# Turning q, k and y1 by 32x32 blocks on VectorE and by way of DRAM, in place of TensorE's transposes

## The reference

```python
def pool_layer(x, norm_g, w_in, w_pool, pool_scale, w_out):
    h = rms_norm(x, norm_g)
    u, z = jnp.split(h @ w_in, 2, axis=-1)
    y = pool_mixer(u, w_pool, pool_scale) * jax.nn.silu(z)
    return x + y @ w_out

def moba_layer(x, norm_g, w_in, q_norm, k_norm, w_out):
    h = rms_norm(x, norm_g)
    q, k, v, z = jnp.split(h @ w_in, 4, axis=-1)
    q = rope(rms_norm(heads(q), q_norm))
    k = rope(rms_norm(heads(k), k_norm))
    v = heads(v)
    o = moba_attention(q, k, v).transpose(0, 2, 1, 3).reshape(B, S, D_INNER)
    return x + (o * jax.nn.silu(z)) @ w_out
```

## Time and profile before

| | us |
|---|---|
| median of 3 runs | 430.5 (430.43 to 430.61) |
| the profiled execution | 432.63 |
| its span | 430.8 |
| TensorE (PE) busy | 423.2 |
| VectorE (DVE) busy | 285.3 |
| ScalarE (ACT) busy | 230.6 |
| GpSimd (POOL) busy | 128.4 |

### The profile page before, as it was taken

How to read it: one execution, slowest core, us unless ns; L and a number is a source line. 1 busy time by engine, 2 the same in 40 slices (tenths; PEclk the granted TensorE clock), 3 DMA queues, 4 the chain that set the end, 5 groups by cost and what they waited for, 6 DMA issues and landing times.

```text
span 430.8 us, 5669 instructions
## 1 busy us (share of the span) xinstructions
PE 423.2 (98%) x2214; PEld 363.1 (84%) x2214; DVE 285.3 (66%) x354; ACT 230.6 (54%) x406; POOL 128.4 (30%) x97
## 2 busy tenths in 40 slices
PE   6999999999999999999999999999999999999997
PEld 6989898988888888888878888888888888888885
DVE  1979987779875545356664798447983579836532
ACT  3935553535354443478448765577654786546310
POOL 0157000000000000079904595055940559300000
PEclk9999999999999999999999999999999999999999
DMA  8986869464555747436933567336672355731002
GB/s 271 384 282 214 272 207 342 160 210 142 195 196 153 227 129 218 124 92 208 300 111 99 173 183 236 93 98 194 192 213 86 98 196 195 241 108 43 2 0 97
DMA packets 38026, 75.25 MB, mean 175 GB/s; under 512 B 1648, under 2 KB 1776, under 8 KB 38000
## 3 DMA queue, kind: packets, MB, share of 16 engines
q1 hardware_dynamic: 37280, 73.83, 53.0%
q10 hardware_dynamic: 720, 1.07, 0.7%
HBM read 73.84 MB, written 1.05 MB: 174 GB/s over the span
## 4 chain that ended last, share of the span: by engine, by line
PE 89%; POOL 7%; DMA 2%; ACT 1%; DVE 0%; issue 0%; ACTq 0%
PE acc L579 23%; PE acc L581 23%; PE acc L580 23%; PE aux L634 3%; POOL wide L326 3%; PE acc L602 3%; PE acc L624 3%; PE acc L621 3%; PE acc L623 3%; PE aux L718 2%; DMA wide<-in_xT_dram 2%; POOL k_s L319 1%; PE aux L725 1%; PE aux L737 1%; PE aux L736 1%; PE aux L735 1%
## 5 line engine op out<-in xcount | busy, mean ns | idle before, releaser
L816 DVE TENSOR_TENSOR w_lo<-raw,w_hi 128x2048 fp32r<-128x2048 f32 x65 | 160.2, 2470 | 55.9 <-ACT w_hi L349 55.8
L349 ACT ACTIVATE w_hi<-raw 128x2048 fp32r<-128x2048 f32 x64 | 122.1, 1917 | 40.4 <-PE acc L581 27.6
L579 PE MATMUL acc<-w_hi,hT_hi 128*128 128x512 f32 x320 | 127.7, 399 | 0.0
L581 PE MATMUL acc<-w_hi,hT_lo 128*128 128x512 f32 x320 | 125.0, 391 | 0.0
L580 PE MATMUL acc<-w_lo,hT_hi 128*128 128x512 f32 x320 | 124.8, 390 | 0.0
L581 PEld LDWEIGHTS acc<-w_hi,hT_lo 128*128 128x128 f32 x320 | 60.1, 188 | 12.9
L580 PEld LDWEIGHTS acc<-w_lo,hT_hi 128*128 128x128 f32 x320 | 60.3, 188 | 11.6
L579 PEld LDWEIGHTS acc<-w_hi,hT_hi 128*128 128x128 f32 x320 | 60.2, 188 | 11.5
L579 PE MATMUL acc<-w_hi,aT_hi 128*128 128x512 f32 x160 | 63.7, 398 | 0.0
L581 PE MATMUL acc<-w_hi,aT_lo 128*128 128x512 f32 x160 | 62.5, 391 | 0.0
L580 PE MATMUL acc<-w_lo,aT_hi 128*128 128x512 f32 x160 | 62.4, 390 | 0.0
(11 more groups left out here) (125 smaller groups left out, 568.4 us busy)
## 6 DMA issues: line engine op xcount, KB each, us to landing
raw<-in_w_in_dram SPq DMA_DIRECT2D x46, 1024.0 KB, 5.4
raw<-in_w_out_dram SPq DMA_DIRECT2D x16, 1024.0 KB, 5.0
raw<-in_w_pool_dram SPq DMA_DIRECT2D x4, 1024.0 KB, 5.5
raw<-in_w_in_dram SPq DMA_DIRECT2D x8, 256.0 KB, 8.0
wide<-in_xT_dram ACTq DMA_DIRECT2D x4, 256.0 KB, 7.6
xs<-in_x_dram SPq DMA_DIRECT2D x1, 1024.0 KB, 8.5
out_dram<-ysb SPq DMA_DIRECT2D x4, 256.0 KB, 2.1
wide<-in_table_dram SPq DMA_DIRECT2D x1, 256.0 KB, 8.2
```

The costliest lines, as they stand in the source:

```text
L349: act.activation(w_hi[:, slot, :], raw[:, slot, :], ACT.Copy).then_inc(hi_made, 1)
L579: pe.matmul(a, shi, whi, start=first and k == 0, stop=False)
L581: ins = pe.matmul(a, slo, whi, start=False, stop=last and k == GK - 1)
L816: dve.tensor_tensor(w_lo[:, slot, :], raw[:, slot, :], w_hi[:, slot, :].bitcast(F32), ALU.subtract).then_inc(w_split, 1)
```

## The change

- **q, k** no longer pass TensorE and PSUM. VectorE does the rope (`rope`: two products with the sine table, one with the cosine table, the sum) and then turns the 32x32 blocks in place of each (`blocks`, a transpose instruction over 128 x 1024). SP stores the tile to DRAM (`between`) and loads it back in four DMAs of 32 partitions that put the blocks in their places (`move_blocks`). For k the result is used as it lies, through a view with runs of 32; for q ScalarE copies it into `qT` (`lay_q`).
- **GpSimd** keeps the reciprocal roots alone; k's scaling goes to ScalarE (`scale_k`, 8 instructions per group). The negated q root is made by GpSimd once per group, not by VectorE per head.
- **y1** of groups 0 to 2 takes the same way (`y1_turn`, `move_y1`). Its split (`y1_hi`, `y1_lo`) moves one group later; that of group 2 stands in the tail, at j == 1. Group 3's y1 is turned by TensorE as before.
- **Weight loads** from the sixth granule of layer 1 on are issued by ScalarE, two granules ahead, in front of `weight_hi`. SP's queue holds the moves.
- TensorE's waits change with it: scores wait for `kT_landed` and `qT_made`, and `y_needed` for whole groups.

```diff
+Q = 32
+MOVED = 16 * (P // Q)
...
+ACT_LOADS = N_L1 + 5
...
-        qT, kT = qkT[:, 0], qkT[:, 1]
+        qT = qkT[:, 0]
+        kT = qkT[:, 1].rearrange("p h s -> p (h s)").rearrange("p (a t h i) -> p t h a i", a=P // Q, t=TT, h=HPG)
+        y1_blocks = uT[:, :, :].rearrange("p f s -> p (f s)")[:, 0:TT * COLS]
...
+        y1T = y1_blocks.rearrange("p (a t h i) -> p a t h i", a=P // Q, t=TT, h=HPG)
...
+        between = [nc.dram_tensor(f"between{i}", (P, TT * COLS), F32, kind="Internal").ap() for i in range(3)]
...
+        def y_tiles(dst, g, t):
+            return dst[:, HPG * g:HPG * (g + 1), t * P:(t + 1) * P].rearrange("p h (a i) -> p h a i", i=Q)
...
+            def move_blocks(dst, blocks, between, times, stored, landed):
+                if times:
+                    sp.wait_ge(landed, MOVED * times)
+                sp.dma_start(between, blocks).then_inc(stored, 16)
+                sp.wait_ge(stored, 16 * (times + 1))
+                quadrants = between.rearrange("(a j) (b n) -> b j a n", j=Q, n=2 * P)
+                for b in range(P // Q):
+                    sp.dma_start(dst[b * Q:(b + 1) * Q, :].rearrange("j (a n) -> j a n", n=2 * P),
+                                 quadrants[b]).then_inc(landed, 16)
+            def flat(buf):
+                return buf.rearrange("p t n -> p (t n)")
+            def move_q(g):
+                sp.wait_ge(qk_blocked[0], g + 1)
+                move_blocks(flat(scratch[0]), flat(scratch[0]), between[0], g, qk_stored[0], qkT_landed[0])
+            def move_k(g):
+                sp.wait_ge(qk_blocked[1], g + 1)
+                sp.wait_ge(scores_ready, HPG * g)
+                move_blocks(flat(qkT[:, 1]), flat(scratch[1]), between[1], g, qk_stored[1], qkT_landed[1])
+            def move_y1(g):
+                sp.wait_ge(y1_blocked, g + 1)
+                move_blocks(y1_blocks, y1_blocks, between[2], g, y1_stored, y1T_landed)
+            for n in range(N_L1, ACT_LOADS):
+                load(n % RING, layer1_weights(n), n)
             for g in range(GROUPS):
-                for j in range(8):
-                    src = w_in1_v[:, (j % 2) * GK:(j % 2 + 1) * GK, bass.ds((j // 2) * D_INNER + g * COLS, COLS)]
-                    load(j % RING, src, N_L1 + 8 * g + j)
-            for i, (h, q) in enumerate(OUT1_ORDER):
-                load(i % RING, w_out1_v[:, q * GK:(q + 1) * GK, h * COLS:(h + 1) * COLS], N_OUT1 + i)
+                move_q(g)
+                move_k(g)
+                if g > 0:
+                    move_y1(g - 1)
...
-            def norm_rope(g, i):
-                v = qk[i]
...
-                    for t in range(TT):
-                        ins = pool.tensor_tensor(v4[:, t], v4[:, t],
-                                                 k_rstd[:, t, :].unsqueeze(2).to_broadcast([P, HPG, HEAD_DIM]),
-                                                 ALU.mult)
-                    chain.done(ins)
...
-                ins.then_inc(rope_parts[i], 1)
...
+                if ACT_LOADS <= n + 2 < N_END:
+                    act.wait_ge(w_split, n - 1)
+                    act.dma_start(raw[:, (n + 2) % RING, :].rearrange("p (k n) -> p k n", k=GK),
+                                  layer1_weights(n + 2)).then_inc(raw_landed[(n + 2) % RING], 16)
...
+                    act.wait_ge(qk_blocked[which], g)
...
+                    if g > 0:
+                        act.wait_ge(qkT_landed[which], MOVED * g)
...
-            def qkT_out(g, i):
-                for b in range(2):
-                    act.wait_ge(qk_turned[i], 2 * g + b + 1)
-                    dst = (qT, kT)[i]
-                    act.activation(dst[:, 2 * b:2 * b + 2, :].rearrange("p h s -> p (h s)"), aux[2 * i + b][:, :],
-                                   ACT.Copy).then_inc(qkT_made[i], 1)
+            def scale_k(g):
+                act.wait_ge(k_rstd_made, g + 1)
+                for t in range(TT):
+                    for h in range(HPG):
+                        tile = k_s[:, t, h * HEAD_DIM:(h + 1) * HEAD_DIM]
+                        ins = act.activation(tile, tile, ACT.Copy, scale=k_rstd[:, t, h:h + 1])
+                ins.then_inc(k_scaled, 1)
...
+            def lay_q(g):
+                act.wait_ge(qkT_landed[0], MOVED * (g + 1))
+                act.wait_ge(scores_ready, HPG * g)
+                moved = scratch[0].rearrange("p t n -> p (t n)").rearrange("p (a t h i) -> p t h a i", a=P // Q, t=TT,
+                                                                           h=HPG)
+                for t in range(TT):
+                    act.activation(qT[:, :, t * P:(t + 1) * P].rearrange("p h (a i) -> p h a i", i=Q), moved[:, t], ACT.Copy).then_inc(qT_made, 1)
             def y1_hi(g):
+                act.wait_ge(y1T_landed, MOVED * (g + 1))
+                for t in range(TT):
+                    act.activation(y_tiles(aT_hi, g, t), y1T[:, :, t].rearrange("p a h i -> p h a i"),
+                                   ACT.Copy).then_inc(y_hi, 1)
...
+                scale_k(g)
                 w(5)
                 qkv_evacuate(g, 2, not attend)
+                if g >= 2:
+                    y1_hi(g - 2)
                 w(6)
-                qkT_out(g, 0)
+                lay_q(g)
                 w(7)
                 tanh_z(g, not attend)
-                if attend:
-                    y1_hi(g - 1)
-                qkT_out(g, 1)
 
             h1_hi(1)
...
                     probs_out(last, j - 1)
-            y1_hi(last)
+                if j == 1:
+                    y1_hi(last - 1)
+            y1_hi_last()
...
-                for i in range(2):
-                    pe.wait_ge(qkT_made[i], 2 * (g + 1))
-                if h < 2:
-                    pe.wait_ge(y_split, 8 + 2 * g)
+                pe.wait_ge(qT_made, TT * (g + 1))
+                pe.wait_ge(qkT_landed[1], MOVED * (g + 1))
+                if HPG * g + h < 2:
+                    pe.wait_ge(h_split, 4)
                 else:
                     pe.wait_ge(exp_made, HPG * g + h - 1)
                 s = aux[h % 2]
-                pe.matmul(s[:, 0:P], qT[:, h, 0:P], kT[:, h, 0:P], start=True, stop=True)
-                pe.matmul(s[:, P:3 * P], qT[:, h, P:SEQ], kT[:, h, :], start=True, stop=True).then_inc(scores_ready, 1)
+                pe.matmul(s[:, 0:P], qT[:, h, 0:P], kT[:, 0, h], start=True, stop=True)
+                pe.matmul(s[:, P:3 * P], qT[:, h, P:SEQ], kT[:, :, h], start=True, stop=True).then_inc(scores_ready, 1)
...
-            def turn_qk(g, i, first):
-                pe.wait_ge(roped[i], g + 1)
-                if first:
-                    pass
-                elif i == 0:
-                    pe.wait_ge(exp_made, HPG * g)
-                else:
-                    pe.wait_ge(y1_made, HPG * g)
-                turn((2 * i, 2 * i + 1), qk[i], qk_turned[i])
-            def turn_y1(g, after_q):
-                pe.wait_ge(y1_made, HPG * (g + 1))
-                if after_q is not None:
-                    pe.wait_ge(qkT_made[0], 2 * (after_q + 1))
-                turn((0, 1), y1, y_turned)
...
-                    if j == 6:
-                        turn_qk(g, 0, first)
-                    if j == 7:
-                        if not first:
-                            turn_y1(g - 1, g)
-                        turn_qk(g, 1, first)
...
-                    pe.wait_ge(y_split, 8 + k // 2 + 1)
+                    pe.wait_ge(y_split, 8 + (k // 2 + 1 if k >= HPG * last else 2 * (k // HPG) + 2))
...
-            def rope_sum(g, i):
-                dve.wait_ge(rope_parts[i], g + 1)
-                dve.tensor_tensor(qk[i], qk[i], scratch[i], ALU.add).then_inc(roped[i], 1)
+            def blocks(dst, src):
+                return dve.transpose(dst.rearrange("p (b n i) -> p n b i", b=P // Q, i=Q),
+                                     src.rearrange("p t n -> p (t n)").rearrange("p (n b i) -> p n b i", b=P // Q, i=Q))
+            half = HEAD_DIM // 2
+            def rope(g, i):
+                if i == 0:
+                    dve.wait_ge(summed[0], g + 1)
+                else:
+                    dve.wait_ge(k_scaled, g + 1)
+                v4 = qk[i].rearrange("p t (h d) -> p t h d", h=HPG)
+                s4 = scratch[i].rearrange("p t (h d) -> p t h d", h=HPG)
+                for a, b in ((0, half), (half, 0)):
+                    tab = rope_tab[:, 2 * i + 1, :, a:a + half].unsqueeze(2).to_broadcast([P, TT, HPG, half])
+                    ins = dve.tensor_tensor(s4[:, :, :, a:a + half], v4[:, :, :, b:b + half], tab, ALU.mult)
+                chain.done(ins)
+                tab = rope_tab[:, 2 * i, :, :].unsqueeze(2).to_broadcast([P, TT, HPG, HEAD_DIM])
+                chain.done(dve.tensor_tensor(v4, v4, tab, ALU.mult))
+                chain.done(dve.tensor_tensor(qk[i], qk[i], scratch[i], ALU.add))
+                blocks(scratch[i].rearrange("p t n -> p (t n)"), qk[i]).then_inc(qk_blocked[i], 1)
+            def y1_turn(g):
```

(66 more changed lines are left out.)

27 lines of the change are left out of this document (15 added, 12 removed).

## The result

The changed kernel takes **449.62 us** (median of 4 runs, 449.07 to 455.97) against 430.53 before: ratio 1.046, 95% interval 1.041 to 1.050. Slower by 19 us; the forecast was 423.6, faster. The runs of this kernel lie further apart than those of the one before; every ratio here leaves out runs more than 1.5% above their kernel's fastest, which the profiled run, 455.97 (span 454.0), just is.

What follows compares the result with a forecast made beforehand. TensorE was taken as the bound, busy 423.2 of 430.8 us. Turns removed -10.5, tail wait +2.9 and ScalarE's queue +0.7 sum to -6.9 us: 430.5 - 6.9 = 423.6 us, range 421.0 to 428.5.

Steps and rivals of the forecast that it cites:

- What leaves TensorE: In TensorE's stream, the turns of q, k and groups 0 to 2's y1 go, taking 10.5 us off.
- The wait in the tail: Before the third granule of layer 1's output product, TensorE waits for group 2's y1 split: 2.9 us lost.
- ScalarE's queue: Weight-load issues of 0.45 us delay the probabilities' copy at six places, 0.12 us each: 0.7 us lost, bounds 0 to 1.3.
- VectorE and GpSimd: VectorE gains 9.4 us of work per group, block turn 1.23, weight low parts 2.29; GpSimd loses most work; no gain booked.
- k's way over DRAM: k's store and four loads before the scores take 7.5 us, landing 2.6 us early in group 3; no loss booked.
- in layer 1 the DMA engines are half idle: The prediction's argument, from its profile rows, against slow moves that make TensorE wait before head 0's scores.
- Rival D: Slow moves stall TensorE before head 0's scores in every group; m us per move loses 4m - 44.6; slower; chance 0.09.

Runs made afterwards that it cites:

- e1: The changed kernel run once more, unedited, for a second profile; 447.55 us, ratio 1.038.
- e2: The changed kernel with only the first half of each of ScalarE's 35 weight loads brought in; 426.08 us, ratio 0.990.
- e5: The changed kernel with ScalarE laying q out after the high part of the group's last weight granule instead of before it; 443.64 us, ratio 1.022.
- e6: The changed kernel with k's move (store and four fetches) issued by GpSimd on its own queue; 453.66 us, ratio 1.046.
- e9: The changed kernel with four of each group's eight weight loads halved, those just ahead of and beside k's move; 428.29 us.
- e10: The changed kernel with the other four of each group's eight weight loads halved, none of them beside k's move; 434.49 us.
- e12: The changed kernel with weight loads alone on SP's queue and all three moves (q, k, y1) issued by GpSimd; 447.52 us, ratio 1.035.
- e4: The changed kernel with k turned by TensorE again, q and y1 still moved over DRAM; 429.46 us, ratio 0.9965.
- e7: e4 with group 2's y1 split earlier in the tail, before head 1's exponentials and maximum; 424.90 us, ratio 0.987.
- e8: e7 with the weight loads back on SP's queue and the moves of q and y1 issued by GpSimd; 427.12 us, ratio 0.989.
- e11: e8 with VectorE's block turn of y1 and the earlier group's y1 low part put 2.25 us earlier; 425.39 us, ratio 0.988.
- e3: The kernel before with only layer 1's weight loads put on ScalarE's queue, no moves; 431.97 us, ratio 1.0034.

## Why the prediction was wrong

The profiles can be added up. The base is the span of the kernel before at its median, 430.5 - 1.8 = 428.7, less the turns. Half clock: the time at 0.50 by the granted clock's records while TensorE works, halved.

| us | turns | scores wait | tail wait | half clock | ScalarE's queue | sum | span |
|---|---|---|---|---|---|---|---|
| changed | -10.5 | 20.9 | 2.9 | 10.3 | 1.4 | 453.7 | 454.0 |
| e1 | -10.5 | 13.9 | 2.9 | 7.4 | 1.4 | 443.8 | 444.4 |
| e2 | -10.5 | 0 | 2.9 | 1.7 | 1.4 | 424.2 | 423.7 |
| e5 | -10.5 | 9.6 | 3.5 | 3.2 | 1.4 | 435.9 | 436.6 |
| e6 | -10.5 | 19.6 | 2.9 | 9.7 | 1.4 | 451.8 | 452.2 |
| e9 | -10.5 | 0.4 | 2.9 | 0 | 1.4 | 422.9 | 423.1 |
| e10 | -10.5 | 5.3 | 2.9 | 4.6 | 1.4 | 432.4 | 432.4 |
| e12 | -10.5 | 13.5 | 4.6 | 9.3 | 0 | 445.6 | 445.9 |
| e4 | -7.0 | 0 | 2.9 | 1.7 | 1.4 | 427.7 | 427.4 |
| e7 | -7.0 | 0 | 0 | 0 | 1.4 | 423.1 | 422.9 |
| e8 | -7.0 | 0 | 2.2 | 1.7 | 0 | 425.6 | 425.8 |
| e11 | -7.0 | 0 | 2.0 | 0 | 0 | 423.7 | 423.9 |

(-7.0: 10.5 less the 4 x 0.87 of k's turns, which TensorE makes again; the late sum of group 0 stays away.)

- *What leaves TensorE, 10.5 us*: right. 88 turns are gone; laid over the kernel before product by product, e1 gains 10.6 us at the turns, and the sums close within 0.7 us.
- *The wait in the tail, 2.9 us*: right to the tenth, and for the reason given where y1 landed in time (in e2 it lands at 376.7 and the copy for the probabilities ahead of its split ends at 378.0); e7 takes it away by order alone. In e5 and e12 the late landing set it, 3.5 and 4.6 us. What it can trigger was not booked: 1.7 us of half clock.
- *ScalarE's queue, 0.7 us*: the mechanism is right, the size is not; e3 measures 1.4, near the upper bound of 1.3. The six places cost 0.20 us each and not 0.12. An issue takes 0.37 us, not 0.45, but the slack was smaller than the 0.33 read from the earlier trace rows: TensorE needs 0.05 of it, and the weight load that stood 0.2 ahead of the product now starts with it.
- *VectorE and GpSimd*: right. The block turn measures 1.25 us (1.23 booked), low parts 2286 ns (2.29 booked, 2470 before), GpSimd 32 us busy.
- *k's way over DRAM, booked at nothing*: **this is the step that failed.** Its start and its deadline were right: from the store's issue to the last landing that costs nothing the forecast had 10.1 us in group 3 and 11.5 in the others, and e1 has 11.4 and 12.0 to 12.9. The move was not 7.5 us but 18.2, 15.5, 16.7 and 12.3 in the four groups. The prices came from transfers with little beside them. What excused this, "in layer 1 the DMA engines are half idle", is a mean over 50 us; in the stretch in which the forecast placed the move the share was 0.82, and in group 0's 0.87, before any move was added.
- *Rival D* named place and mechanism, with a chance of 0.09. Its formula, with e1's moves (62.7 us in all), gives 62.7 - 44.6 = 18.1 us of waits; they were 13.9, for the deadlines lie up to 1.4 us later than reckoned. With 13.9 it is 423.6 + 13.9 = 437.5; of the 10 us up to 447.55 the clock is 7.4 and the queue 0.7, and the profiled run is 1.2 under the median. D had no term for the clock, and that made it too mild.

The clock is the second cause. In the profiles of layer 1 and the tail all 15 waits of TensorE from 3.5 to 6.6 us came with a stretch at 0.50, of 3.4 to 10.2 us; of the 14 from 2.0 to 3.1 us ten did (2.9 us in e4: yes; 2.9 us in e9: no). In e1 that is 14.9 us of working time. The Trainium skill (TensorE: Matmul & The Clock Gate, Loop structure matters more than you think) warns of this, matmuls that run at the low clock after a long wait for a DMA; the trace agrees.

## What to carry to other kernels

Before a transfer is put on a path that TensorE waits for, read the DMA share in the very microseconds of the transfer, not over the stage, and price it as one that shares full engines with what is in flight: here 2.6 us of store (e2) became 5.8 to 8.6. A stop of a saturated TensorE can cost more than its length: 7.4 on 16.8 us in e1, 1.7 on 2.9 in e4, nothing on 3.3 in e9. Waits that end an overlap may show only in the weight loads' row, not in the matmuls'. Of this change, what paid was moving only what has slack (q, y1) and splitting y1 before its consumer's chain: e7, 424.90 us, 1.3% under the kernel before (one of its six runs took 427.93).

## What the runs showed of the hardware

- A third queue does not speed a transfer in full engines: 453.66 us with k on GpSimd's queue (e6), 447.55 without. The first packet of k's store comes 2.0 to 4.0 us after its issue in e6, 2.1 to 4.4 in e1, and 0.8 in e2, where the weight loads are halved.
- The weight loads are held up by the moves in turn: they land in 7.7 us on ScalarE's queue, in 5.6 on the same queue without moves (e3).
- ScalarE's sequencer issues ahead of its engine: the load of 212.84 goes out as the first of the two copies ahead of it starts (212.83), and yet an issue sets the engine back: the next high part starts 0.48 us after the instruction ahead of it in e3, 0.12 in the kernel before.
- GpSimd's issue of a fetch takes 0.55 us (e8) against 0.43 on SP (e1), and its store reached DRAM in 3.0 us (e8).
